# Two transformer blocks on one core: the second mixer's differential norm on one packed bank, with its gate sigmoids a slab later

## What is computed

```python
def _diff_attention(...):                 # 8 heads, two softmaxes each, head width 128
    w = a[:, :, 0] - lam * a[:, :, 1]     # difference of the two softmaxes
    o = einsum(w, v)
    o = _rmsnorm(o, subln_g) * (1.0 - lam_init)     # over the 128 numbers of a head

def _rmsnorm(x, g):
    return x * rsqrt(mean(square(x)) + EPS) * g

def _mixer(...):
    o_a = _diff_attention(...)
    o_b = _mla(...)                       # 8 heads of a second, latent attention
    g = sigmoid(h @ w_in[gates] + b_gate) # 2048 gate columns: g_a and g_b
    return (g_a * (o_a @ w_branch_diff) + g_b * (o_b @ w_branch_mla)) @ w_out
```

## Time and profile before

| what | value |
|---|---|
| time, median of 3 runs | 2604.66 us (2604.38 to 2609.56) |
| time of the profiled execution | 2605.08 us |
| its span, first to last instruction | 2603.1 us |
| PE busy | 2518.7 us, 97% of the span |
| DVE, ACT, POOL busy | 1002.7, 365.6, 130.6 us |
| mean granted clock of PE | 0.993 of full speed |
| chain that ended last | PE 90%, DVE 4%, DMA 3%, ACT 2% of the span |

### The profile page before, as it was taken

One profiled execution on the slowest core, in us unless ns is written; L12 is line 12 of the kernel. 1 busy time (PEld: TensorE's weight loads), 2 busy tenths in 40 slices (PEclk: granted clock), 3 DMA queues, 4 the chain that ended last, 5 costly groups with the idle time before them and its releaser, 6 DMA issues.

```text
span 2603.1 us, 74060 instructions
## 1 busy us (share of the span) xinstructions
PE 2518.7 (97%) x33806; PEld 2146.4 (82%) x33806; DVE 1002.7 (39%) x1856; ACT 365.6 (14%) x842; POOL 130.6 (5%) x114
## 2 busy tenths in 40 slices
PE   8999999999999999999999999999999999999998
PEld 8966778887698577876994778769999998999997
DVE  5663464633477734444666235440000001000002
ACT  1001241210100023401000234120000001000000
POOL 0000000000100001400000014010000000000000
PEclk9999999999999999999999999999999999999999
DMA  6445242013444542345435323579999999999996
GB/s 260 148 144 196 105 146 110 4 59 130 146 170 150 194 166 82 130 166 209 164 114 197 140 104 129 232 259 368 426 427 426 426 426 401 426 427 426 426 425 256
DMA packets 58054, 607.72 MB, mean 233 GB/s; under 512 B 7365, under 2 KB 7493, under 8 KB 12353
## 3 DMA queue, kind: packets, MB, share of 16 engines
q1 hardware_dynamic: 52272, 587.74, 56.7%
q0 software_dynamic: 5648, 18.04, 2.1%
HBM read 599.66 MB, written 6.09 MB: 233 GB/s over the span
## 4 chain that ended last, share of the span: by engine, by line
PE 90%; DVE 4%; DMA 3%; ACT 2%; issue 1%; SPq 0%; DVEq 0%; ACTq 0%
PE bank L2804 19%; PE bank L314 16%; PE bank L470 16%; PE bank L2817 10%; PE bank L497 7%; PE bank L324 5%; PE bank L1676 3%; PE bank L1798 3%; DMA slot<-in_experts 3%; PE bank L1244 2%; PE bank L1662 1%; DVE arena L2517 1%; PE bank L972 1%; PE bank L2736 1%; PE bank L1267 1%
## 5 line engine op out<-in xcount | busy, mean ns | idle before, releaser
L2804 PE MATMUL bank<-arena,slot 128*64 128x84 f32 x14336 | 540.9, 236 | 12.9 <-issue 7.3
L2804 PEld LDWEIGHTS bank<-arena,slot 128*64 128x64 f32 x14336 | 527.4, 137 | 19.2 <-issue 17.2
L314 PE MATMUL bank<-h_cm,slot 128*128 128x256 f32 x1472 | 324.1, 381 | 0.4 <-ACT h_cm L361 0.2
L314 PEld LDWEIGHTS bank<-h_cm,slot 128*128 128x128 f32 x1472 | 280.1, 191 | 44.4 <-issue 6.5
L3003 DVE TENSOR_TENSOR ff<-ff,bank 128x168 f32<-128x168 f32 x112 | 36.9, 330 | 638.8 <-PE bank L2804 634.6
L2817 PE MATMUL bank<-ff,arena 128*64 128x84 f32 x5376 | 212.8, 238 | 7.6 <-issue 7.2
L2817 PEld LDWEIGHTS bank<-ff,arena 128*64 128x64 f32 x5376 | 202.0, 138 | 13.4 <-issue 13.4
L470 PE MATMUL bank<-arena 128*128 128x128 f32 x1584 | 187.8, 275 | 1.1 <-DVE arena L560 1.1
L470 PEld LDWEIGHTS bank<-arena 128*128 128x128 f32 x1584 | 182.2, 192 | 1.3 <-DVE arena L560 1.3
L314 PE MATMUL bank<-arena,slot 128*128 128x256 f32 x608 | 133.3, 380 | 2.3 <-DVE arena L2520 2.3
L470 PEld LDWEIGHTS bank<-h_cm,slot 128*128 128x128 f32 x1056 | 123.1, 195 | 10.2 <-issue 10.2
(11 more groups left out here) (474 smaller groups left out, 2899.6 us busy)
## 6 DMA issues: line engine op xcount, KB each, us to landing
slot<-in_experts SPq DMA_DIRECT2D x112, 2048.0 KB, 16.1
arena<-in_experts SPq DMA_DIRECT2D x84, 1024.0 KB, 11.8
slot<-in_ffn SPq DMA_DIRECT2D x22, 2048.0 KB, 8.3
x_tm<-in_experts SPq DMA_DIRECT2D x28, 1024.0 KB, 11.6
slot<-in_ffn SPq DMA_DIRECT2D x22, 1024.0 KB, 4.9
slot<-in_dense SPq DMA_DIRECT2D x11, 2048.0 KB, 7.8
slot<-in_dqk SPq DMA_DIRECT2D x8, 2048.0 KB, 7.7
slot<-in_g SPq DMA_DIRECT2D x8, 2048.0 KB, 7.7
```

What stands on the lines that cost most here:

```text
L314: ins = pe.matmul(ps[0:m, j * S:(j + 1) * S], w[:, k * width + c0:k * width + c0 + m], rhs[:, k, :], start=k == 0, stop=k == ks - 1)
L2804: ins = pe.matmul(bank[64 * c:64 * c + 64, m * PLACES:(m + 1) * PLACES], weights[:, c0:c0 + 64], CURRENT[:, k, :], start=k == 0, stop=k == ...
```

## The change

The norm's sums of squares go to one bank: PE multiplies each pair of heads with 32 columns of ones, into 32 partitions of it. DVE takes that bank to `OA_INVERSE`, the first 512 columns of `QD`, with the factor `1 - lam_init` worked into the mean and eps; ACT takes the root of 512 columns and DVE their reciprocal. PE then spreads the result back to 128 partitions with four `head_spread` products in four banks, and DVE multiplies `OA` with bank and gain in one instruction a bank. `oa_stages` counts five steps a layer. PE's wait for the reciprocal stands in front of `bm`, its wait for the finished `OA` between `bm` and `bd` as before.

On ACT each gate sigmoid `g2(0)`, `g2(1)` comes one softmax later, and the root stands between `g2(1)` and the copies for `mla_out(1)`. On DVE only the first bank of a gate slab goes ahead of the wait for the exponentials, and the last slab's four banks are summed after the reciprocal.

```diff
+        OA_INVERSE = QD[:, 0:2, :].rearrange("p k s -> p (k s)")
...
 def pool_extras(pool, l):
-            pool.wait_ge(named("oa_stages"), 4 * l + 1)
+            pool.wait_ge(named("oa_stages"), 5 * l + 1)
...
 def pe_mixer2(pe, l):
             g2(2)
-            pe.wait_ge(named("oa_stages"), 4 * l + 1)
+            pe.wait_ge(named("oa_stages"), 5 * l + 1)
+            ps = fill(pe, ("dn", l), next_bank())
             for b in range(4):
-                ps = fill(pe, ("dn", l, b), next_bank())
-                filled(pe.matmul(ps[:, :], ones, QD[:, 2 * b:2 * b + 2, :], start=True, stop=True), ("dn", l, b))
+                ins = pe.matmul(ps[32 * b:32 * b + 32, :], ones[:, 0:32], QD[:, 2 * b:2 * b + 2, :], start=True, stop=True)
+            filled(ins, ("dn", l))
             mla_turn(1)
             pe_gate_seven(pe, l, 3, SEVEN[0:4])
             mla_out(1)
             pe_gate_seven(pe, l, 3, SEVEN[4:7])
+            pe.wait_ge(named("oa_stages"), 5 * l + 4)
+            for b in range(4):
+                head_spread(pe, ("dnb", l, b), b, OA_INVERSE)
...
-            pe.wait_ge(named("oa_stages"), 4 * l + 4)
+            pe.wait_ge(named("oa_stages"), 5 * l + 5)
...
 def act_mixer2(act, ch, l):
-            g2(0)
             diff_out(3)
             act_softmax(act, l, "mla", 0, 12 * l + 8)
             for a in range(4):
                 drained(act, ("do", l, a))
             act.activation(QD, OA, ACT.Square).then_inc(named("oa_stages"), 1)
-            g2(1)
+            g2(0)
             mla_out(0)
             act_softmax(act, l, "mla", 1, 12 * l + 10)
+            g2(1)
+            act.wait_ge(named("oa_stages"), 5 * l + 2)
+            act.activation(OA_INVERSE, OA_INVERSE, ACT.Sqrt).then_inc(named("oa_stages"), 1)
+            mla_out(1)
             g2(2)
-            mla_out(1)
-            act.wait_ge(named("oa_stages"), 4 * l + 2)
-            act.activation(QD, QD, ACT.Sqrt).then_inc(named("oa_stages"), 1)
             g2(3)
...
 def dve_mixer2(dve, ch, l):
-            mla_weights(0, lambda: gate(1, 0, 1))
-            gate(1, 2, 3)
+            mla_weights(0, lambda: gate(1, 0))
+            gate(1, 1, 2, 3)
             mla_turned(0)
-            mla_weights(1, lambda: gate(2, 0, 1))
-            gate(2, 2, 3)
-            for b in range(4):
-                ps = full(dve, ("dn", l, b))
-                free(v.tensor_scalar(QD[:, 2 * b:2 * b + 2, :], ps[:, :].rearrange("p (k s) -> p k s", s=S), 1.0 / P, EPS,
-                                     ALU.mult, ALU.add), ("dn", l, b))
-                drained(dve, ("dn", l, b))
+            mla_weights(1, lambda: gate(2, 0))
+            gate(2, 1, 2, 3)
+            ps, kept = full(dve, ("dn", l)), (0.2 + 0.6 * math.exp(-0.3 * l)) ** 2
+            ins = v.tensor_scalar(OA_INVERSE, ps[:, :], 1.0 / (P * kept), EPS / kept, ALU.mult, ALU.add)
+            free(ins, ("dn", l))
+            drained(dve, ("dn", l))
             dve.sem_inc(named("oa_stages"), 1)
             mla_turned(1)
-            gate(3, 0, 1)
-            dve.wait_ge(named("oa_stages"), 4 * l + 3)
-            ch.step(v.reciprocal(QD, QD))
-            init = 0.8 - 0.6 * math.exp(-0.3 * l)
-            ch.step(v.tensor_tensor(OA, OA, QD, ALU.mult))
-            v.tensor_scalar(OA, OA, col(f"subln{l}"), 1.0 - init, ALU.mult, ALU.mult).then_inc(named("oa_stages"), 1)
-            gate(3, 2, 3)
+            dve.wait_ge(named("oa_stages"), 5 * l + 3)
+            v.reciprocal(OA_INVERSE, OA_INVERSE).then_inc(named("oa_stages"), 1)
+            gate(3, 0, 1, 2, 3)
+            for b in range(4):
+                ps = full(dve, ("dnb", l, b))
+                part = OA[:, 2 * b:2 * b + 2, :]
+                ins = v.scalar_tensor_tensor(part, ps[:, :].rearrange("p (k s) -> p k s", s=S), col(f"subln{l}"), part,
+                                             ALU.mult, ALU.mult)
+                free(ins, ("dnb", l, b))
+            for b in range(4):
+                drained(dve, ("dnb", l, b))
+            dve.sem_inc(named("oa_stages"), 1)
```

## The result

The change made the kernel slower: 2615.50 us (median of 6 runs, 2614.41 to 2623.03) against 2604.32 (6 runs, 2604.13 to 2609.56), a ratio of 1.0045 with a 95% interval of 1.0032 to 1.0059. The forecast was 2592.0. The profiled execution after took 2618.48 us, its span is 2616.4.

The account below looks back on a forecast made before the run. PE, busy for 97% of the span, was taken as the bound. Gains of 5.85 us in layer 0 and 6.85 in layer 1, together 12.7, off 2605.08 gave 2592.4; the median 0.42 lower, 2592.0, range 2590 to 2595.

Parts of the forecast that it names:

- The waits and the order: Mixer: PE's waits at lines 2162, 2188, 2200 and `bd` vanish, worth 5.18 us in layer 0, 5.48 in layer 1.
- The packed sums: Norm in the mixer: PE's eight records shrink from 3.44 to 1.00 us, 2.44 us a layer off PE's path.
- the spread: Norm in the mixer: new products on PE's path, costing 1.07 us a layer, 3.44 without overlap.
- the dense layer: Start of layer 0's dense layer: PE waits for DVE's line 2629 to read bank 0, costing 0.7 us.
- What is late next: Mixer after the change: scaling done by 1084.1, copies 4.2 us and reciprocal 9 us ahead of PE's need; no cost.
- hold the scaling up to the end of its sums: Rival at `mla_turn(1)`: POOL's sums delay DVE's scaling, PE waits 0.8 us a layer, time 2593.6; 1 in 10.
- The sum in the mixer: Waits plus packed sums less spread and dense-layer cost: 5.85 us in layer 0, 6.85 in layer 1, together 12.7.
- the wait at `bd`: Mixer: PE's wait for the finished `OA` goes through the shorter reciprocal, worth 1.2 + 0.17 us a layer.
- the bank turn: Bank use moves on by one a layer, so PE's dense layer opens 0.7 us later, layer 0 only.
- Does the gain reach the end?: Experts: their load stream sets the pace but starts earlier by what PE gained, so the end moves by the 12.7 us.
- The rival that had the experts swallow the gain: Experts' load stream doesn't start earlier, so all gain is lost: 2604.7; 4 in 100.
- The rival that could: Slower: chain of sums, root and copies over PE, DVE, ACT stops PE at `mla_out(1)`; 2607.7 at 12 us; 3 in 100.

Follow-up runs that it names:

- order_alone: The kernel before with only the new order on ACT and DVE, the norm still on four banks, no PE instruction changed; 2593.76 us, ratio 0.9956.
- before_pad34: The kernel before, mixer untouched, with 34 more waiting instructions at the head of PE's program; 2629.43 us, ratio 1.0099.
- after_skip222: The changed kernel with 217 never-executed waits in a branch, PE's program 256 instructions longer ahead of the experts' loop than before; 2594.35 us, ratio 0.9957.
- after: The kernel with the whole change, 34 PE instructions longer ahead of the experts' loop than the kernel before; 2615.50 us, ratio 1.0045.

## Why the prediction was wrong

*The waits and the order: right.* All four waits fell in both layers. `order_alone` shows 5.23 and 5.55 us for the order by itself, where the prediction had 5.18 and 5.48 for the four waits.

*The packed sums, the spread, the dense layer: right.* 0.99 us (forecast 1.00), 1.07 (1.07), and at the dense layer PE waited 1.41 us for DVE's line 2639, the 0.73 of before and the 0.7 of the forecast:

```profile
1211.11 3.84 PE L470 MATMUL bank<-h_cm,slot 128*128 128x128 f32 x32 [1.41 <-DVE arena L2639]
```

*What is late next: right.* The timelines of DVE and ACT after the change:

```profile
1078.68 5.44 DVE L2485 TENSOR_TENSOR arena<-arena,ff 128x512 f32<-128x512 f32 x2
...
1086.78 0.68 DVE L2515 TENSOR_SCALAR arena<-bank 128x512 f32<-128x512 f32 x1
...
1088.23 3.34 DVE L2521 RECIPROCAL arena<-arena 128x512 f32<-128x512 f32 x1
```

```profile
1081.44 1.28 ACT L2381 ACT_TABLE_LOAD   x1
1087.56 0.63 ACT L2381 ACTIVATE arena<-arena 128x512 f32<-128x512 f32 x1 [4.83 <-DVEq L2518]
1088.09 1.05 ACT L2333 COPY arena<-bank 128x512 f32<-128x512 f32 x2
```

The scaling under POOL's sums ended at 1084.1, as forecast, by some luck: it took 5.44 us, not 4.88, and began 0.5 us earlier than I had it; the copies for `mla_out(1)` ended at 1089.1, 5.9 us before PE's start there, the reciprocal at 1091.6. POOL did not hold the scaling up to the end of its sums, 1086.3. The table load ran while ACT still waited, so the root came 1.3 us sooner than I had it.

*The sum in the mixer: right, one term in two places.* From `mla_scores(0)` to `bd` it went from 72.46 to 66.11 and from 72.78 to 66.10 us, 6.35 and 6.68 less, where I had 6.55 and 6.85 ahead of the 0.7. But I booked the wait at `bd`, 1.37 us a layer, to the packing, and each part removes it by itself: the packing on top of the order is worth 1.12 and 1.13 us, together 2.25, of which the bank turn takes 0.7 back. The sums and the spread alone would give 2.44 - 1.07 = 1.37 a layer; the products ahead of the packed sums and of the spread take 0.10 us longer to the next start, and `mla_turn(1)` 0.06.

*Does the gain reach the end? This step failed.* I asked only whether the loads would start earlier, and took the length of the experts' stage as given. The loads did start earlier: the first of line 3122 (now 3132) was issued at 1686.19, before at 1698.35, 12.2 us. PE even waited for them less (0.5 us, before 4.3), but with the code back in its place it waited 4.3 again, so that is no gain of the earlier start. The stage grew by 23.6 us all the same, because the 34 instructions that the change adds to PE moved the loop's code; `before_pad34` shows it without the mixer, `after_skip222` shows the change without it. The rival that had the experts swallow the gain was no nearer: it let them hide it behind the loads, and nothing in it could make the kernel slower. The rival that could would have shown as a wait at the second `mla_out`, and PE had none there. A longer stage stood among the signs of being wrong, without a cause that would bring it. That the rows of the stage before would hold (a DMA share of 1.01) I read as a limit by the loads; what the trace of before shows as well, that PE's code needed no fetch there, I did not look at.

With the code back in its place the change takes 2594.35 us, inside the range given. Against the 2603.48 of before beside it, the ratio's interval means a gain of some 7.5 to 15 us, which holds the 12.7 of the forecast, so the last 2.35 us can't be told from noise. In the profiled execution a loss lies ahead of the experts: from PE's line 2559 to the first product it took 38.7 us there (1699.41 to 1738.09), and 36.4 before (1710.97, by its line 2549, to 1747.32), with a granted clock of 0.85 against 0.92 in the 42 us before the product; why it was lower is open. Of the 23.6 us, 16.6 are waits (PE's waits behind the first expert product add up to 36.8 us after and 20.2 before), and an estimated 4.2 are the clock, half of the 5.2 and 3.2 us behind the two gaps. The rest is not settled.

## What to carry to other kernels

Where a long loop closes a kernel, instructions added anywhere ahead of it on the same engine move its code: before the price of an edit is summed up, compare the instruction packets in the loop's stretch, and count in which block the loop starts and ends. A loop that fetches nothing can be one edit from the step, as this one was, 17 to 34 instructions away. When a stage that the edit did not touch changes its length, give the engine the same number of idle instructions in the old kernel; that run shows whether the place of the code is the cause, and one with the code moved back shows what the edit is worth without it. Of the two halves of this change, the order alone brings all that can be measured (0.44%, against 0.43% for the whole with the code in its old place), without one instruction more on PE.

## What the runs showed of the hardware that was not expected

The experts' inner loop jumps back over more than six blocks of code: over its 28 rounds the page counts 21,504 products and as many weight loads, 1536 instructions a round, and waits come on top. Before the change it did so for 680 us without one instruction packet, while 34 instructions more brought 27 packets and gaps of up to 8.9 us. After the change too it ran without a packet from 1990 to 2160 and from 2220 to 2365, between the outer loop's turns. The Trainium skill (Runtime: NRT & Kernel Launch, "Instruction fetch mechanics") says that a taken branch whose target lies outside a window of two blocks has to fetch it; the trace of before disagrees, with no packet from 1800 to 2480, and the measurement decides. The Trainium skill (Advanced Engine Details and Errata, "ISA Cache") gives TensorE 128 KB in lines of 16 KB, which would be eight, and in the same list says "Only 2 cache lines!". Two do not go with the trace of before. An estimate from the eight, that seven blocks and the next one fit and eight blocks and the next do not, would give such a step, and nine packets a turn as counted; no run here shows what is held.

Nine packets are small beside the loads (0.15 MB of 22.54 from 1930 to 1990), yet the first and the third turn cost 8.6 to 8.9 us of idle time each, in `after` and in `before_pad34`, and within that idle time the granted clock falls from 2.4 to 1.2 GHz. At the second turn of `after`, where PE goes on to the late gate, the gaps stay at 2.1 us or less and the clock stays up. Why the first gap is so much longer than a packet takes (the nine from 1930 to 1990 took 1.1% of 16 engines' 60 us, some 1.2 us each) is open. An instruction that only waits on a semaphore met long ago held PE up by about 0.1 us: 180 of them put the first product back by 16.4 us, past the 9.34 us for which PE waits there in any case.
